# A hybrid attention step on one core: decode units at other places between the projection's pieces, and stick-breaking scores in token order

## What is computed

```
h = rmsnorm(x); u = h @ w_in            # 1152 tokens x 1024 -> 4104 columns
fox:  p = softmax(q.k/8 + cumulated log forget)          (8 heads of 64)
stick-breaking:  z = q.k/8                               (8 heads of 64)
      a = sigmoid(z) * product over later keys of (1 - sigmoid(z))
y = rmsnorm(o_a)*silu(z_a) , rmsnorm(o_b)*silu(z_b);  x + [y_a, y_b] @ w_out;  final rmsnorm
```

## Time and profile before

| what | value |
|---|---|
| median of the runs | 1256.26 us |
| profiled execution, its span | 1253.29 us, 1251.5 us |
| TensorE matmul busy | 1105.0 us (88%) |
| VectorE busy | 722.9 us (58%) |
| ScalarE busy | 452.7 us (36%) |
| GpSimd busy | 207.4 us (17%) |
| mean granted clock of TensorE | 0.963 |

### The profile page before, as it was taken

One profiled execution on the slowest core, in us unless ns is written; L12 is line 12 of the kernel. 1 busy time (PEld: TensorE's weight loads), 2 busy tenths in 40 slices (PEclk: granted clock), 3 DMA queues, 4 the chain that ended last, 5 costly groups with the idle time before them and its releaser, 6 DMA issues.

```text
span 1251.5 us, 28539 instructions
## 1 busy us (share of the span) xinstructions
PE 1105.0 (88%) x12001; PEld 932.9 (75%) x12001; DVE 722.9 (58%) x1000; ACT 452.7 (36%) x787; POOL 207.4 (17%) x153
## 2 busy tenths in 40 slices
PE   5899899889799989978889899999988878878997
PEld 5888798778687878767678787777776656656886
DVE  4433544155154545565576725666679999874553
ACT  4412132112112214323033335656564544433331
POOL 3100000000000001110011116100033343335460
PEclk9999999999899999989889999999989999989999
DMA  7382566796788786969869797234422413112332
GB/s 197 98 232 59 155 195 207 288 322 187 260 280 289 300 296 202 310 245 312 214 260 317 275 280 228 68 77 101 93 51 43 77 32 62 38 73 68 102 134 84
DMA packets 152033, 222.52 MB, mean 178 GB/s; under 512 B 92264, under 2 KB 128104, under 8 KB 135536
## 3 DMA queue, kind: packets, MB, share of 16 engines
q1 hardware_dynamic: 131184, 201.98, 52.5%
q10 hardware_dynamic: 20736, 18.88, 4.4%
HBM read 197.17 MB, written 23.66 MB: 176 GB/s over the span
## 4 chain that ended last, share of the span: by engine, by line
PE 63%; issue 12%; DVE 11%; DMA 9%; ACT 4%; POOL 1%; ACTq 0%; DVEq 0%; SPq 0%; POOLq 0%
PE bank L716 20%; PE bank L1510 7%; PE bank L789 6%; PE bank L1012 5%; PE bank L1056 5%; PE bank L1032 4%; DMA v_ring<-in_cache_fox_v 4%; PE bank L829 3%; PE bank L993 3%; PE bank L1071 2%; DVE k_buf L612 2%; DMA v_ring<-in_cache_sb_v 2%; DVE q_cur L605 2%; PE bank L818 2%; DMA x_in<-in_x_prompt 1%
## 5 line engine op out<-in xcount | busy, mean ns | idle before, releaser
L716 PE MATMUL bank<-w_hi,hT_hi 128*128 128x256 f32 x1152 | 343.1, 298 | 6.1 <-ACT u_out L435 5.8
L716 PE MATMUL bank<-w_hi,hT_lo 128*128 128x256 f32 x1152 | 331.9, 288 | 1.9 <-issue 1.9
L716 PE MATMUL bank<-w_lo,hT_hi 128*128 128x256 f32 x1152 | 332.7, 289 | 0.0
L716 PEld LDWEIGHTS bank<-w_hi,hT_hi 128*128 128x128 f32 x1152 | 228.0, 198 | 18.4 <-issue 12.4
L716 PEld LDWEIGHTS bank<-w_lo,hT_hi 128*128 128x128 f32 x1152 | 228.1, 198 | 0.0
L716 PEld LDWEIGHTS bank<-w_hi,hT_lo 128*128 128x128 f32 x1152 | 227.5, 197 | 0.0
L435 ACT ACTIVATE u_out<-bank 128x256 f32<-128x256 f32 x144 | 55.3, 384 | 449.5 <-PE bank L716 431.5
L612 DVE STREAM_TRANSPOSE k_buf<-k_buf 128x2048 f32<-128x2048 f32 x64 | 144.0, 2285 | 19.3 <-DMA k_buf<-in_cache_fox_k 19.1
L1265 POOL TENSOR_TENSOR pr<-pr,om 128x1023 f32<-128x1023 f32 (+3 forms) x64 | 81.0, 1268 | 247.5 <-DVE om L1210 244.2
L1210 DVE TENSOR_TENSOR_SCAN om<-om 128x1024 f32<-128x1024 f32 (+3 forms) x64 | 114.2, 1785 | 2.9 <-ACT om L1145 2.2
L1032 PE MATMUL bank<-ident,pr 128*128 128x128 f32 x576 | 89.7, 282 | 23.7 <-DVE pT L1233 21.5
(11 more groups left out here) (168 smaller groups left out, 1697.2 us busy)
## 6 DMA issues: line engine op xcount, KB each, us to landing
k_buf<-in_cache_fox_k SPq DMA_DIRECT2D x32, 1024.0 KB, 9.9
v_ring<-in_cache_fox_v SPq DMA_DIRECT2D x32, 1024.0 KB, 7.2
k_buf<-in_cache_sb_k SPq DMA_DIRECT2D x32, 1024.0 KB, 8.8
v_ring<-in_cache_sb_v SPq DMA_DIRECT2D x32, 1024.0 KB, 8.1
w_raw<-in_w_in SPq DMA_DIRECT2D x15, 1024.0 KB, 14.8
out<-u_out ACTq DMA_DIRECT2D x72, 128.0 KB, 5.5
k_nat<-out SPq DMA_DIRECT2D x32, 256.0 KB, 3.9
q_nat<-q_scratch SPq DMA_DIRECT2D x32, 256.0 KB, 4.7
```

What stands on the lines that cost most here:

```text
L716: mm = pe.matmul(bank[:, U + i % 2, 0:NCOL], a[:, k, hcols(s)], b[c % 2][:, k, :], start=(k == 0 and n == 0), stop=(k == KD - 1 and n == 2))
```

## The change

Three things, all in the overlap stage.

1. The tables move. The places (piece numbers) of each unit's steps, n = 0 to 15:

| | before | changed |
|---|---|---|
| scores | 30 43 53 60 67 74 81 88 96 102 107 113 119 124 130 136 | 33 43 53 60 67 73 80 87 94 100 105 111 116 122 128 133 |
| turn_p | 33 50, then scores + 2 (fox), + 4 (sb) | 36 50, then the same distances |
| values of chunks 0 to 3, fox from unit 2 | scores + 3, 3, 4, 5 | scores + 4, 4, 5, 7 |
| values, sb | scores + 5, 5, 6, 7 | scores + 6, 6, 7, 8 |
| turn_o | scores + 6 (fox), + 8 (sb) | scores + 8 (fox), + 9 (sb) |

2. In sb units TensorE writes its scores into PSUM with a step of 16 elements, so that they lie in token order. The sigmoids then read and write contiguously. The second sigmoid (`d_p`) moves from `scores` to `soften`, behind the copy of one more piece.

3. The first load of keys is called chunk by chunk at pieces 10 to 13 and not at once at piece 10.

```diff
-        SCORES_AT = [30, 43] + [53 + 7 * k for k in range(DB - 2)] + [96, 102, 107, 113, 119, 124, 130, 136]
-        TURN_P_AT = [33, 50] + [s + (2 if n < DB - 2 else 4) for n, s in enumerate(SCORES_AT[2:])]
-        VALUES_AT = [47] + [s + 1 for s in TURN_P_AT[1:]]
+        SCORES_AT = [33, 43, 53, 60, 67, 73, 80, 87, 94, 100, 105, 111, 116, 122, 128, 133]
+        TURN_P_AT = [36, 50] + [s + (2 if n < DB - 2 else 4) for n, s in enumerate(SCORES_AT[2:])]
+        VALUES_AT = [(47, 47, 48, 49), (52, 52, 53, 54)] + [
+            (s + 2, s + 2, s + 3, s + 5) if n < DB - 2 else (s + 2, s + 2, s + 3, s + 4) for n, s in enumerate(TURN_P_AT[2:])]
...
-                if i in (10, 24):
-                    load_first(0 if i == 10 else 1)
+                if i in (10, 11, 12, 13, 24):
+                    load_first(i - 10 if i < 24 else CH)
...
-                        if i == VALUES_AT[n] + (0, 0, 1, 2)[v]:
+                        if i == VALUES_AT[n][v]:
                             values(n, v)
-                    if i == VALUES_AT[n] + 3:
+                    if i == VALUES_AT[n][CH - 1] + 1:
                         turn_o(n)
...
+            def sigmoid(dst, sign, done):
+                act.activation(dst[:, 0:PAST], flat(bank[:, DSC:DSC + CH, :]), ACT.Sigmoid, scale=sign).then_inc(done, 1)
+                act.activation(dst[:, PAST:KEYS], bank[:, DNEW, 0:DS], ACT.Sigmoid, scale=sign).then_inc(done, 1)
+
             def soften(n):
                 if n >= DB:
+                    act.wait_ge(dpt_ready, NC1 * n)
+                    sigmoid(d_p, SCALE, dss_done)
                     return
...
-                act.wait_ge(dpt_ready, NC1 * n)
-                past = bank[:, DSC:DSC + CH, :].rearrange("p r (t s) -> p r t s", s=32)
-                for dst, sign, done in ((d_om, -SCALE, dsig_done), (d_p, SCALE, dss_done)):
-                    act.activation(dst[:, 0:PAST].rearrange("p (r s t) -> p r t s", r=4, s=32), past, ACT.Sigmoid,
-                                   scale=sign).then_inc(done, 1)
-                    act.activation(dst[:, PAST:KEYS], bank[:, DNEW, 0:DS], ACT.Sigmoid, scale=sign).then_inc(done, 1)
+                sigmoid(d_om, -SCALE, dsig_done)
...
-                                mm = pe.matmul(bank[32 * j:32 * j + 32, DSC + r, :], q_t[rows_r, half, h, :],
-                                               k_buf[rows_r, :, at:at + 32], start=(g == 1 and hh == 0 and half == 0),
+                                out = bank[32 * j:32 * j + 32, DSC + r, :]
+                                if g:
+                                    out = out.rearrange("m (s t) -> m t s", s=32)
+                                mm = pe.matmul(out, q_t[rows_r, half, h, :], k_buf[rows_r, :, at:at + 32], start=(g == 1 and hh == 0 and half == 0),
```

More of the change, by code:

```diff
@@ L358, in forget, with load_k @@
                                          ).then_inc(ln_loaded, 16)
-            def load_k(n):
-                for c in range(CH):
+            def load_k(n, cs=range(CH)):
+                for c in cs:
                     sp.dma_start(k_buf[:, 4 * c:4 * c + 4], cache_chunk(K_IN[n // DB], n, c)).then_inc(kd_loaded[c], 16)
@@ L368, in load_first @@
             def load_first(part):
-                if part == 0:
+                if part < CH:
                     sp.wait_ge(htp_ready, 2 * T)
-                    load_k(0)
+                    load_k(0, (part,))
                 else:
```

## The result

The changed kernel took 1269.06 us in the median (1262.36 to 1273.08, 7 runs), against 1258.14 us (1253.2 to 1264.12, 7 runs) for the kernel before on the same chip. The ratio is 1.007, with a 95% interval of 1.0039 to 1.0102: a loss of under 1%, within the predicted range, 10 us above the predicted 1259. The profiled execution took 1270.06 us against 1253.29, which is near the lowest run of the kernel before, so the profiles lie 16.8 us apart where the medians lie 10.9.

The account below looks back on a forecast made before the run. TensorE was taken to set the end, with DMA and VectorE close behind. The terms summed to +2.6 us; 1253.3 profiled, plus 2.6, plus 3.0 to the median, gave 1259 us, range 1228 to 1288.

Parts of the forecast that it names:

- First scores: Pieces 30 to 33: TensorE's wait of 4.0 us for `c_hl` goes; −4.0 us.
- Fox values: Value chunks of fox units, used later: TensorE's waits for their loads fall from 19.3 to 12.9 us; −6.4 us.
- `d_pT` and `o_d`: TensorE's waits for these two buffers in the overlap stage go; −8.4 and −15.1 us.
- `oT_s`: Five units where `turn_o` and next `turn_p` share a piece: copy waits of about 0.6 us each; +0.6 us.
- Turned keys: Sb scores five pieces apart, and unit 9: waits for turned keys of 10.0 us for 2.6; +7.4 us.
- Sb values behind the next keys: Units 10, 12, 15: chunk 3 loads issued behind the next load; waits of 5.9, 13.1, 12.5 us; +31.5 us.
- Clock: TensorE at 1.2 GHz after waits, some 1.5 us lost each; two fewer waits in all; −3 us.
- Strided scores: Sb scores written to PSUM with a step of 16: taken as 0, up to 32 us in eight units.
- The rival at 1291 us: Eight sb units' scores, written with a step, take 1.89 times as long; +32 us, 1291 us; chance 20%.
- Second sigmoid and first keys in four calls: Sb sigmoid one piece later, covered by VectorE's scan; first key loads split in SyncE's queue, changing nothing; 0.
- The rival of late loads that cost little: Sb value loads issued late share the DMA engines and cost little; 1227 us without the 31.5 us; chance 28%.
- VectorE as the bound: At five-piece distances with the weights' split, VectorE's chain outlasts TensorE's work; +11 more, 1270 us; chance 8%.

Follow-up runs that it names:

- three-value kernel: Changed kernel with only the value steps of units 9, 11 and 14 one piece earlier; 1223.92 us, ratio 0.9721 to the kernel before.

## Why the prediction held, and where its terms did not

- **First scores.** −4.0 for `c_hl`: the wait is gone, and it is back where the old fox places are.
- **Fox values.** 12.9 us were forecast and 5.8 measured, in two places (3.35 at unit 0, 2.42 at unit 2). The 2.4 us each of units 3 and 7 did not come, and unit 2's were 2.4 and not 4.3. The bound from one landing was too pessimistic by 7 us.
- **`d_pT` and `o_d`.** −8.4 and −15.1 were forecast. `d_pT` has left the list, `o_d` has 3.0 left. The kernel with the old sigmoids has 10.4 there and the one with the old places 2.8, so most of it is the work of the changed sigmoids and not of the places. Whether their length or their order in ScalarE's queue did it, no kernel separates.
- **`oT_s`.** +0.6 was forecast, +3.9 measured (6.3 for 2.4).
- **Turned keys.** +7.4 was forecast, +12.7 measured: four places as said, of 2.52 (unit 9), 3.06, 3.32 and 6.41 us (units 10, 12 and 15). The last was forecast at 3.5 at most. In the kernel with only the value steps moved the four are 2.52, 0.96, 1.44 and 2.55, 7.5 in all. The scores of these units did not start any sooner for it. From the start of `turn_p` to the scores it is 8.0, 8.3 and 11.4 us in the changed kernel (units 10, 12, 15) and 7.8, 8.3 and 11.4 in the other, where the 1.95 us of values, and at unit 15 1.91 us of waiting for `d_pT`, lie within that time. VectorE's chain sets these starts in both. It was sized too short, at unit 15 above all: 6.4 us of wait and not 3.5.
- **Sb values behind the next keys.** +31.5 was forecast, as 5.9, 13.1 and 12.5 us; 31.2 came, as 4.85, 16.07 and 10.30. This was the deciding term, and it was right in its places and its cause; that the sum agrees to 0.3 us is luck, since the single waits missed by −1.0, +3.0 and −2.2. The three-value kernel takes all three waits away and brings one of 4.9 us at unit 12, and the one with the later weights takes away the share of the weights.
- **Clock.** This step failed. I took −3, from the number of waits. Over the sb part 61 us ran at 1.2 GHz and not 34. In all, the waits from unit 0's scores to the end of the overlap stage grew by 10.6 us (fox stretch and the first scores −12.3, sb part +22.9), and the remaining 6.2 of 16.8 us are slower work: 2.8 us up to the end of the overlap stage and 3.4 after it, whose cause stays open. The waits' number had hardly changed, but their lengths had. 13 us of the 46 that the three-value kernel wins in the sb part are in TensorE's busy time, not in its waits. The working had a second fault: it took the missing 0.06 of the mean clock as lost time, 16.6 us. The mean also counts the time in which TensorE waits. Between the changed kernel and the three-value one that way of counting would give some 25 us, and TensorE's work became 13 us shorter.
- **Strided scores.** 0 was forecast and 4.46 us a unit measured where no wait stood ahead, as before. The rival at 1291 us is out. The Trainium skill's rule in "PSUM — Partial Sum Buffer" (Specifications), that a non-contiguous pattern slows matmuls significantly, does not hold for this form here: float32 results of 32 partitions by 512 elements, step of 16 elements. The rule may hold for others; none was run.
- **Second sigmoid and first keys in four calls.** Both were costed at 0. No kernel isolates them. Nothing in the lists of waits names either.

The profiled executions lie 16.8 us apart and the medians 10.9, where the sum said 2.6. Against the 16.8, the fox values were 7.1 us too pessimistic, and `oT_s` 3.3, the turned keys 5.3 and the clock with what it stands for 9.2 too kind. The 3.5 us left are in `o_d` and in gaps without a releaser. So the forecast came near in part because a term that was too dark stood against several that were too kind, and the range had room for the rest. The rival of late loads that cost little is refuted by the waits themselves. That of VectorE as the bound has a share of truth: its chain sets when the scores of units 10, 12 and 15 start. But it is not what the changed kernel lost by: moving three value steps gives back 46 us, with VectorE's work unchanged.

## What to carry to other kernels

Where one queue serves a ring and a large buffer, look at what a step's place does to the order of issue and not only to the work between steps: one piece earlier or later decides whether a 1 MB load stands ahead of 4 MB or behind them. Write down for each load what stands ahead of it in its queue, and compare its landing with the work left until it is wanted. Count by the time a load holds the DMA engines and not by its bytes: here 1 MB of weights held them for some 11 us. And count a long wait of TensorE above its own length: here 33 us of waits took another 13 us with them.

## What was not expected of the hardware

A long gap in front of TensorE was followed by work at the lower of its two levels, 1.2 GHz, and this was dearer than I had counted. How dear varied: behind the same wait of 6.41 us the scores of unit 15 took 5.84 us in the kernel with the later first loads. In the changed kernel the scores of unit 15 waited 6.41 us for turned keys, and then took 6.94 us where undisturbed ones take 4.46:

```profile
706.38 6.94 PE L794 MATMUL bank<-k_buf,q_cur 32*32 32x512 f32 x128 [6.41 <-DVE k_buf L614]
```

The clock was 0.59 over the 8 us behind the 10.30 us wait, and back at 1.00 in the next 10:

```profile
736.00:744.00 8.00, 7.39 (x65) 6.29 (x65) 0.64 (x3) 0.38 (x1) 0.00 (x0) 0.59 0.85 331
744.00:754.00 10.00, 9.76 (x130) 9.46 (x131) 1.76 (x4) 1.97 (x4) 0.00 (x0) 1.00 0.13 47
```

Next, ScalarE's sigmoid of 128 x 2048 elements took 3717 ns where it wrote to memory with steps and read PSUM in another order, and 1882 ns over contiguous data, while no cost was measured of TensorE's writing its results to PSUM with a step of 16 elements.
